# State space layer: the time-step projection in fp32 on four token quarters, and the first two x tiles as a pair

## The reference, cut to what matters

```python
zxbcdt = h @ in_w
z, xbc, dt = split(zxbcdt)                          # dt: 32 columns, one a head
xbc = silu(causal_dwconv(xbc, conv_w, conv_b))      # 4 taps along the tokens
dt = softplus(dt + dt_bias)
a_neg = -exp(a_log)
# chunks of 128 tokens, 4 groups of 8 heads
acum = cumsum(dt * a_neg, axis=1)                   # inside a chunk
scores = (c @ b.T) * exp(acum[t] - acum[s])         # causal
y = scores @ (xs * dt) + exp(acum) * (c @ state)
state = state * exp(acum[-1]) + b.T @ (xs * dt * exp(acum[-1] - acum))
```

## Time and profile before

| | us |
|---|---|
| median of 3 runs | 2979.68 |
| lowest, highest | 2976.48, 2985.04 |
| profiled execution | 2974.77 |
| its span | 2973.1 |
| PE busy in it | 2874.2 |
| DVE busy | 1849.2 |
| ACT busy | 1045.2 |
| mean granted clock of TensorE | 0.987 |

### The profile page before, as it was taken

The page is one execution under the profiler, slowest core; times in us unless marked ns, Lnnn a source line. Parts: engine busy times, 40 slices in busy tenths (PEclk is TensorE's granted clock), DMA queues, the critical chain, the costliest instruction groups (busy, mean ns, idle before and its releaser), DMA issues.

```text
span 2973.1 us, 40383 instructions
## 1 busy us (share of the span) xinstructions
PE 2874.2 (97%) x16384; PEld 2273.8 (76%) x16384; DVE 1849.2 (62%) x2043; ACT 1045.2 (35%) x1344; POOL 464.9 (16%) x502
## 2 busy tenths in 40 slices
PE   4998999999999999999999999999999999999989
PEld 4886667777888888888867888888777886777667
DVE  6567647762754555543487748667868246677683
ACT  4124445652411111111234424334434124445452
POOL 3002010001111111110101103021212002333340
PEclk7999999999999999999999999999999999999999
DMA  7454011101333333321114233243521321212111
GB/s 241 142 160 112 6 29 30 30 23 43 93 114 112 106 106 108 110 92 50 44 50 145 76 95 107 71 138 121 173 86 57 114 98 37 72 36 72 56 63 60
DMA packets 248826, 258.65 MB, mean 87 GB/s; under 512 B 15167, under 2 KB 209392, under 8 KB 248672
## 3 DMA queue, kind: packets, MB, share of 16 engines
q1 hardware_dynamic: 224320, 179.84, 19.8%
q0 software_dynamic: 18768, 59.06, 6.7%
q10 hardware_dynamic: 5584, 17.58, 1.5%
HBM read 223.41 MB, written 30.65 MB: 85 GB/s over the span
## 4 chain that ended last, share of the span: by engine, by line
PE 88%; DVE 6%; ACT 3%; issue 2%; DMA 1%; SPq 0%; POOL 0%; DVEq 0%; ACTq 0%; POOLq 0%
PE PU L1070 17%; PE PU L1072 17%; PE PU L1071 17%; PE PM L1855 2%; PE PU L1084 2%; PE PU L1086 2%; PE PU L1085 2%; PE PU L1833 2%; PE PM L1843 2%; PE PM L1875 2%; PE PU L1444 2%; PE PM L1877 2%; PE PM L1876 2%; PE PU L1368 2%; ACT m_p L2281 1%
## 5 line engine op out<-in xcount | busy, mean ns | idle before, releaser
L1070 PE MATMUL PU<-hH,w_hi_t 128*128 128x512 f32 x1808 | 713.1, 394 | 2.0 <-DVE w_lo_t L2685 1.8
L1072 PE MATMUL PU<-hH,w_lo_t 128*128 128x512 f32 x1808 | 705.0, 390 | 0.0
L1071 PE MATMUL PU<-hL,w_hi_t 128*128 128x512 f32 x1808 | 704.6, 390 | 0.0
L2685 DVE TENSOR_TENSOR w_lo_t<-w_raw,w_hi_t 128x1024 fp32r<-128x1024 f32 x181 | 235.6, 1302 | 260.4 <-ACT w_hi_t L1987 255.3
L1070 PEld LDWEIGHTS PU<-hH,w_hi_t 128*128 128x128 f32 x1808 | 338.6, 187 | 74.3 <-DVE w_lo_t L2685 2.8
L1072 PEld LDWEIGHTS PU<-hH,w_lo_t 128*128 128x128 f32 x1808 | 338.5, 187 | 73.2
L1071 PEld LDWEIGHTS PU<-hL,w_hi_t 128*128 128x128 f32 x1808 | 338.8, 187 | 69.5
L1987 ACT ACTIVATE w_hi_t<-w_raw 128x1024 fp32r<-128x1024 f32 x167 | 174.7, 1046 | 437.1 <-PE PU L1072 328.2
L3238 DVE SCALAR_TENSOR_TENSOR xT<-PU,mod,xT 128x1024 f32<-128x1024 f32 x120 | 153.8, 1282 | 159.4 <-PE PU L1072 159.4
L1025 POOL TENSOR_SCALAR_AFFINE_SELECT s_keep<-s_keep 128x128 f32<-128x128 f32 x128 | 116.7, 929 | 456.6 <-ACT s_keep L2573 456.2
L3564 DVE TENSOR_TENSOR_SCAN s_keep<-s_keep,zero 128x128 f32<-128x128 f32 (+7 forms) x128 | 179.3, 1400 | 2.0 <-POOL s_keep L1025 2.0
(11 more groups left out here) (508 smaller groups left out, 5094.4 us busy)
## 6 DMA issues: line engine op xcount, KB each, us to landing
ada_w<-in_ada_w_dram POOLq DMA_DIRECT2D x64, 384.0 KB, 4.0
w_raw<-in_w_gu_dram SPq DMA_DIRECT2D x44, 512.0 KB, 3.7
w_raw<-in_m_in_w_dram SPq DMA_DIRECT2D x40, 512.0 KB, 3.9
ada_w<-in_w_ada_dram POOLq DMA_DIRECT2D x32, 512.0 KB, 4.7
seg<-decay_sums SPq DMA_DIRECT2D x32, 512.0 KB, 4.2
w_raw<-in_w_down_dram SPq DMA_DIRECT2D x22, 512.0 KB, 3.3
w_raw<-in_w_in_dram SPq DMA_DIRECT2D x17, 512.0 KB, 3.9
ada_w<-in_w_ada_dram SPq DMA_DIRECT2D x16, 512.0 KB, 16.4
```

The lines of the kernel that those rows point to most:

```text
L1070: mm(PU[0:width, up, half, :], whi, aH[:, k, cols], start=k == 0, stop=False)
L1071: mm(PU[0:width, up, half, :], whi, aL[:, k, cols], start=False, stop=False)
L1072: last = mm(PU[0:width, up, half, :], wlo, aH[:, k, cols], start=False, stop=k == kt - 1)
L2685: V.tensor_tensor(w_lo_t[:, p, 0:w], w_raw[:, p, 0:w], w_hi_t[:, p, 0:w].bitcast(F32), ALU.subtract)\
```

## The change

The narrow unit is gone. Its weights (`dt_p`, 128 x 8 x 32) are loaded once, early, by a GpSimd DMA and used in fp32 without a split. `step_columns(k)` gives, for `hH` and `hL` each, four fp32 products of 32 columns by 256 tokens, the four token quarters going to PSUM rows 0, 32, 64 and 96. It stands ahead of each step of `paired`, a function that another layer uses already: at step k tile k of the first unit and, from step 2 on, tile k-2 of the second. The units of the pair are now x tiles 0 and 1. The time-step tables have 128 rows (quarter, head) by 256 tokens in place of 32 by 1024; so there are 4 full transposes in place of 16, and the copies reorder. The bias and `a_log` are loaded four times, one for each quarter, by eight small DMAs. The two stores of decays are made of four DMAs each. ScalarE copies x unit 0 from PSUM to `u_first`, from which VectorE convolves it. All later units and panels change parity.

```diff
 INVERSES = 1 + HEAD_UNITS
-RAW_SCALED = 4
+RAW_SCALED = 5
 W_OUT_ORDER = (0, 1, 2, 3, 4, 6, 7, 5)
...
         y_lo = at("y_lo", A + 4096, [P, 4, T], F32R)
-        dt_w = at("dt_w", A + 4096, [NH, 4, T])
+        dt_w = at("dt_w", A + 4096, [P, 4, 2 * P])
+        dt_p = at("dt_p", A + 13312, [P, KD, NH])
+        u_first = at("u_first", A + 8192, [P, T])
         bt = at("bt", A + 8192, [P, TT, DS])
...
             m_out = a["m_out_w_2"].rearrange("o (k p) c -> p (o k) c", p=P)
-            panel(m_in[:, :, DT0:DT0 + NH], KD, NH)
-
             def tile_decays(i, j):
...
                 else:
-                    sp.wait_ge(a_stored, 32)
+                    sp.wait_ge(a_stored, 128)
                 tile_decays(i, 0)
...
             g.dma_start(d_row[:, :], a["m_d_2"].broadcast_to([P, NH])).then_inc(rp_landed, 16)
+            g.dma_start(dt_p[:, :, :], a["m_in_w_2"].rearrange("o (k p) c -> p (o k) c", p=P)[:, :, DT0:DT0 + NH]).then_inc(rp_landed, 16)
+            for q in range(4):
+                for c, name in ((46, "m_dt_bias_2"), (47, "m_a_log_2")):
+                    g.dma_start(small[32 * q:32 * q + NH, c:c + 1], a[name].rearrange("o h -> h o")).then_inc(rp_landed, 16)
             with counted(g, 8, [(pc, KD), (slab, KD)]) as i:
...
-            def paired(rows, width=P, after={}, over=False):
+            def step_columns(k):
+
+                for n, right in enumerate((hH, hL)):
+                    for q in range(4):
+                        mm(PM[32 * q:32 * q + NH, 2, 0:2 * P], dt_p[:, k, :], right[:, k, 2 * P * q:2 * P * (q + 1)].bitcast(F32),
+                           start=k == n == 0, stop=k == KD - 1 and n == 1)
+
+            def paired(rows, width=P, after={}, over=False, beside=None):
...
                         pe.wait_ge(h_ready, rows + step + 1)
+                        if beside is not None:
+                            if step == 0:
+                                pe.wait_ge(rp_landed, 16 * 12)
+                            beside(step)
                         for half in range(2):
...
             model_norm()
-            feat_pair(hr(), NH)
+            paired(hr(), beside=step_columns)
             hr.next(KD)
...
                 for w, row in enumerate((2, 1)):
-                    for t in range(TT):
-                        last = nc.tensor.transpose(PM[:, 2, w * 256 + t * NH:w * 256 + (t + 1) * NH],
-                                                   dt_w[:, row, t * P:(t + 1) * P], ident[0:NH, 0:NH])
+                    for c in range(2):
+                        last = nc.tensor.transpose(PM[:, 2, w * 256 + c * P:w * 256 + (c + 1) * P],
+                                                   dt_w[:, row, c * P:(c + 1) * P], ident[:, :])
                 last.then_inc(dt_t_s, 1)
-                mm(PM[:, 3, 0:256], ones[0:NH, :], dt_w[:, 0, 0:256], start=True, stop=True).then_inc(dt_t_s, 1)
+                mm(PM[:, 3, 0:256], ones[:, :], dt_w[:, 0, :], start=True, stop=True).then_inc(dt_t_s, 1)
...
                         mid = lambda: group_spread(i - 1)
-                    if i or j:
+                    if i == 0 and j == 3:
+                        mid = lambda: conv_turned(0, 1)
+                    if i or j > 1:
                         feat_unit(panel_ready(), 0, P, KD, hH, hL, mid=mid)
...
                         group_sums(i - 1)
-                    if j:
+                    if i == 0 and j == 2:
+                        conv_turned(0, 0)
+                    elif j and (i or j > 1):
                         conv_turned(i, j - 1)
...
             h_high(m("m_sh", 0, 8))
-            skip()
+
             def step_rates():
...
                 af(dt_w[:, 1, :], dt_w[:, 1, :], ACT.Exp)
-                af(small[0:NH, 40:41], v("a_log", rows=NH), ACT.Exp).then_inc(dt_x, 1)
+                act.wait_ge(rp_landed, 16 * 12)
+                af(small[:, 40:41], small[:, 47:48], ACT.Exp).then_inc(dt_x, 1)
...
                 act.wait_ge(dt_f, 1)
-                act.dma_start(scr_a.rearrange("c h t -> h c t"), dt_w[:, 1, :].rearrange("h (c t) -> h c t", t=P))\
-                    .then_inc(a_stored, 16)
+                def stored(scr, row):
+
+                    for q in range(4):
+                        act.dma_start(scr[2 * q:2 * q + 2, :, :].rearrange("c h t -> h c t"),
+                                      dt_w[32 * q:32 * q + NH, row, :].rearrange("h (c t) -> h c t", t=P)).then_inc(a_stored, 16)
+
+                stored(scr_a, 1)
                 link(af(dt_w[:, 3, :], dt_w[:, 1, :], ACT.Exp))
-                act.dma_start(scr_e.rearrange("c h t -> h c t"), dt_w[:, 3, :].rearrange("h (c t) -> h c t", t=P))\
-                    .then_inc(a_stored, 16)
+                stored(scr_e, 3)
...
                 act.wait_ge(unit_free[n % 2], n // 2 + 1)
+                if i == j == 0:
+                    act.wait_ge(raw_scaled, RAW_SCALED)
                 dst = c_acc[:, j % 2, :] if j < 4 else (bT if j == 4 else cT)[:, :]
...
                 for j in range(6):
-                    split()
+                    if i or j:
+                        split()
                     if i and j == 0:
                         group_gate()
-                    skip()
                     if i == j == 0:
+                        p = unit()
+                        free(af(u_first[:, :], unit_ps(p), ACT.Copy))
+                    else:
+                        skip()
+                    if i == 0 and j == 1:
                         step_rates()
...
                 ffn_body(i, FT // 2 - 9, 0)
-            ve.wait_ge(rp_landed, 48)
+            ve.wait_ge(rp_landed, 16 * 12)
             for hd in range(2):
...
             def step_sizes_1():
-                p = unit()
-                free(V.tensor_scalar(W[0], unit_ps(p, NH), v("dt_bias", rows=NH), None, ALU.add))
-                split()
-                ve.wait_ge(unit_free[p], (uc.n - 1) // 2 + 1)
+                xp, xn = uc.at()
+                ve.wait_ge(unit_done[xp], xn + 1)
+                ve.wait_ge(rp_landed, 16 * 12)
+                link(V.tensor_scalar(W[0], PM[:, 2, 0:2 * P], small[:, 46:47], None, ALU.add))
                 V.scalar_tensor_tensor(W[1], W[0], -1.0, W[0], ALU.mult, ALU.min).then_inc(dt_x, 1)
...
                 link(V.scalar_tensor_tensor(W[2], W[0], 0.0, W[3], ALU.max, ALU.add))
-                link(V.tensor_scalar(W[3], W[2], small[0:NH, 40:41], -1.0, ALU.mult, ALU.mult))
-                for t in range(TT):
-                    tok = slice(t * P, (t + 1) * P)
-                    ins = V.tensor_tensor_scan(W[1][:, tok], ones[0:NH, :], W[3][:, tok], 0.0, ALU.mult, ALU.add)
+                link(V.tensor_scalar(W[3], W[2], small[:, 40:41], -1.0, ALU.mult, ALU.mult))
+                for c in range(2):
+                    tok = slice(c * P, (c + 1) * P)
+                    ins = V.tensor_tensor_scan(W[1][:, tok], ones[:, :], W[3][:, tok], 0.0, ALU.mult, ALU.add)
                 link(ins)
-                V.tensor_tensor(W[0][:, 0:256].rearrange("h (c k) -> h c k", k=NH),
-                                ident[0:NH, 0:NH].unsqueeze(1).broadcast_to([NH, TT, NH]),
-                                W[1][:, P - 1:T:P].unsqueeze(2).broadcast_to([NH, TT, NH]), ALU.mult).then_inc(dt_f, 1)
+                V.tensor_tensor(W[0].rearrange("p (q c k) -> p q c k", q=4, c=2),
+                                ident[:, :].rearrange("p (q k) -> p q k", q=4).unsqueeze(2).broadcast_to([P, 4, 2, NH]),
+                                W[1][:, P - 1:2 * P:P].unsqueeze(1).unsqueeze(3).broadcast_to([P, 4, 2, NH]), ALU.mult).then_inc(dt_f, 1)
...
                 ve.wait_ge(dt_t_s, 1)
-                V.tensor_copy(flat(dt_t), PM[:, 2, 0:256])
-                link(V.tensor_copy(flat(acum), PM[:, 2, 256:512]))
+                for n, dst in enumerate((dt_t, acum)):
+                    ins = V.tensor_copy(dst[:, :, :].rearrange("p (q c) h -> p c q h", c=2),
+                                        PM[:, 2, n * 256:(n + 1) * 256].rearrange("p (c q h) -> p c q h", c=2, q=4))
+                link(ins)
                 ve.wait_ge(dt_t_s, 2)
...
                     ve.wait_ge(x_stored[j % 2], 16 * (2 * i + min(j // 2, 2)))
-                p = unit()
-                u = unit_ps(p)
+                if i == j == 0:
+                    xp, xn = uc.at()
+                    ve.wait_ge(unit_free[xp], xn + 1)
+                    u = u_first[:, :]
+                else:
+                    u = unit_ps(unit())
                 w = lambda tap: vec[:, c_w + 24 * tap + tile:c_w + 24 * tap + tile + 1]
...
                         link(ins)
+                    elif i == j == 0:
+                        ins.then_inc(raw_scaled, 1)
+                        skip()
                     else:
...
                 if i == 0:
+                    split()
                     conv(0, 0)
-                    split()
                     step_sizes_2()
```

14 lines of the change are left out of this document (6 added, 8 removed).

## The result

The changed kernel takes **2989.19 us** (median of 13 runs, 2984.71 to 2995.18), the kernel before 2979.68 (median of 13 on the same chip, 2974.93 to 2985.04): 9.5 us more, ratio 1.0032 with an interval of 1.0023 to 1.0042. The forecast was 6.8 us more, 2986.5.

What follows compares the result with a forecast made beforehand. TensorE was taken as the bound, busy 97% of the span. Terms -2.2 - 2.45 - 0.75 - 1.6 + 10.5 + 1.9 + 1.4 = +6.8 us on 2979.7 gave 2986.5 us, range 2974 to 2996.

Steps and rivals of the forecast that it cites:

- ACT's queue: Behind the time-step tables: six more store issues on ScalarE delay the last table and the conv of C, +1.4 us.
- Projection: In the pair: 48 full-width matmuls go, 64 grouped fp32 products come, with switching costs; net -2.2 us.
- Waits before transposes: TensorE's three waits before transposes of convolved tiles go, since VectorE's time-step work shrinks from 1024 to 256 columns; -2.45 us.
- Tables: Time-step tables: 4 full transposes and a product instead of 16 narrow transposes and a product; -0.75 us.
- the low clock behind them: After the time-step tables: the low-clock spell disappears with full-width tables, -1.6 us; 0 if it stays.
- The lead: Before the fourth x unit: TensorE waits for panel 3's split and the second conv tile; +10.5 us.
- Low clock behind it: After the wait before the fourth x unit: the clock is low following about 10 us idle; +1.9 us.
- Hidden: Extra small DMAs, ScalarE's copy of unit 0 and the split of panel 2 are covered by other work; no time.
- Rival D: Grouped products don't lift the clock, so the pair runs low; whole pair some 14 us, one spell 2; chance 0.08.
- Rival B: In the pair, the column groups don't run side by side; up to +20.5 us, two at a time +6.5; chance 0.13.
- C: The wait for x unit 3 is covered; sum without 10.5 and 1.9 is -5.6, 2974 us; chance 0.15.
- a difference outside 1490 to 1600: Sign that would prove the forecast wrong: time changing outside that stretch of the profile, where no term lies.

Runs made afterwards that it cites:

- Kernels 1 and 2: kernel 1, and kernel 2: the changed kernel with the second conv tile earlier on VectorE alone, ScalarE's order kept; ratio to the kernel before 1.0025.
- Kernel 3: The changed kernel with four decay stores on ScalarE's queue instead of eight; ratio to the kernel before 1.0026.
- kernel 11: The changed kernel with earlier panel and conv tile, four stores, first split behind squares, gathered columns, sixth conv tile before the last table product; 2970.64 us, ratio to before 0.9974.
- kernel 4: The changed kernel with the first x panel's split moved from among the norm's squares to behind them; ratio to the kernel before 1.0015.
- kernel 7: The changed kernel with all four token quarters' fp32 products on the same 32 rows, time steps wrong; ratio to the kernel before 1.0101.
- kernel 1: The changed kernel with the fourth x panel's split (ScalarE, VectorE) and the second conv tile (VectorE) earlier; 2981.5 us, ratio to the kernel before 1.0005.

## Why the prediction was right

Its mechanism, the large term and the sign were right; the sum came out 2.7 us low, by three small terms: the low clock behind the lead, ACT's queue and the start of the stage.

- *Projection, forecast -2.2*: -2.1 in the two profiled executions (44.01 us against 1538.86 - 1491.98 less the 0.79 of the transposes = 46.09), but the other kernels with the same pair took 44.4 to 45.4, so -0.7 to -2.1. All of this scatter is the low clock at the start, which I had called lost with either kernel: with it taken out (1.4 us in the change, 4.25 - 10 x 0.2325 = 1.9 before) it is 42.6 against 44.2, -1.6. That the profiles gave -2.1 is luck. A step took 1519.37 - 1515.38 = 3.99 us, 3.87 to 3.91 by my terms. The records came a little faster than I had them (0.054 us for 0.059), and the price of a change was too small: I had 0.18 us a step from the earlier trace rows, and it is 0.34.
- *Waits before transposes, -2.45*: all three gone.
- *Tables, -0.75, and the low clock behind them, -1.6*: from the fourth tile's transposes to the end of unit C 1574.64 to 1587.46 (0.40 ahead of 1587.86), 12.82 us; before 1565.32 to 1580.53, 15.21. -2.39 for a forecast of -2.35, and no low clock.
- *The lead, +10.5*: 10.32. Kernels 1 and 2 show it to be the order of ACT and DVE, in two parts.
- *Low clock behind it, +1.9*: +2.7 in this execution. Six kernels had the wait of 10.32, and low clock for 2.7 to 5.7 us behind it, half of which is 1.4 to 2.8. 1.9 was a fair middle, and one profile is one draw.
- *ACT's queue, +1.4*: from unit C's end to the first score product 9.18 us against 6.75, so +2.4. The step that failed is the price of an issue, 0.54 us for 0.34 to 0.45: I took single stores, those of the earlier trace rows, for a row of four. The last table ends 15.6 us after the transposes instead of 14.6, and the conv of C starts 2.75 us after its unit is done instead of 0.30. Kernel 3 gave 1.7 us of it back, and kernel 11 took the wait that was left from 0.94 to 0.26.
- *The start of the stage, no term*: +1.05 (kernel 4). Under *Hidden* I followed the copy of unit 0 and the split of panel 2 to their waits; the split of the first panel, which the change widens from 256 to 1024 columns, was not followed at all.
- *Rival D's price* was wrong, without effect on the sum: at 0.43 us for 0.23 a pair of some 31 us at full clock loses some 30 at the lower level, not 14.

Measured: -2.1 - 2.45 - 2.39 + 10.32 + 2.7 + 2.4 + 1.05 = +9.5, for +9.5. Rival B is refuted by the records 0.054 us apart, with kernel 7 beside them, C by the wait itself, D by the full clock from 1496.1 on. The sentence that would have made the prediction wrong, a difference outside 1490 to 1600, held for 1.05 of 9.5 us, and for the 6.6 us more by which the two profiled spans differ, if one takes these instead of the medians.

What the change was worth without the lost lead: kernel 1 takes the stretch to 2.6 us under before, by its median to no measurable difference. The 13 us of its one wait with the clock behind it ate more than all that it saved.

## What to carry to other kernels

When work is merged (two units as a pair, wide steps made narrow), the units in which the other engines' orders are written shift too: look for the first item that an engine now has *behind* something that the bottleneck does late, and move that item, not the work. Three engines idle in turn, each ended by the next, is what that looks like in a profile; here one panel's split and one conv tile, put one place earlier, took 12 us off the stage, more than the 9.5 that the change lost. And follow every instruction whose width changes, even ahead of the stage: beside a busy GpSimd a VectorE operation with both inputs in SBUF cost twice its usual time (2.51 us for 1.23), since it waited for GpSimd's; one with an input in PSUM cost no more (1.28).
